# The S5 recurrence of a Trainium2 block kernel: 15 powered steps replaced by a turned scan, and its output work moved to earlier stages

## What is computed

```python
G, P = 32, 64                                   # channel groups of 16, complex states
dt = jnp.exp(log_dt)[:, None]; mag = jnp.exp(dt * a_re)
abar_re, abar_im = mag * cos(dt * a_im), mag * sin(dt * a_im)
...                                             # bbar = coef * b, complex
bu_re = jnp.einsum("gpc,btgc->tbgp", bbar_re, ug); bu_im = ...
# s[t] = abar * s[t-1] + bu[t], complex, over the 512 tokens
_, _, s_re, s_im = lax.associative_scan(_ssm_combine, (a_seq_re, a_seq_im, bu_re, bu_im), axis=0)
y = einsum("gcp,tbgp->btgc", c_re, s_re) - einsum("gcp,tbgp->btgc", c_im, s_im) + d_skip * ug
zz = gelu(y)
out = zz * sigmoid(zz @ w_glu + b_glu)          # 512 x 512 weights
y_s5 = rms_norm(out) * gain
mix = concatenate([y_rwkv, y_s5]) @ w_out       # 1024 x 1024
```

## Time and profile before

| | us |
|---|---|
| median of 3 runs | 1648.43 (1647.06 to 1651.15) |
| the profiled execution | 1645.37 |
| its span in the trace | 1643.6 |
| busy in the span: TensorE / VectorE / ScalarE / GpSimd | 1492.7 / 805.6 / 584.4 / 269.5 |
| mean granted TensorE clock | 0.959 |

### The profile page before, as it was taken

How to read it: one execution, slowest core, us unless ns; L and a number is a source line. 1 busy time by engine, 2 the same in 40 slices (tenths; PEclk the granted TensorE clock), 3 DMA queues, 4 the chain that set the end, 5 groups by cost and what they waited for, 6 DMA issues and landing times.

```text
span 1643.6 us, 23774 instructions
## 1 busy us (share of the span) xinstructions
PE 1492.7 (91%) x10032; PEld 1155.1 (70%) x10032; DVE 805.6 (49%) x1255; ACT 584.4 (36%) x1012; POOL 269.5 (16%) x225
## 2 busy tenths in 40 slices
PE   6998897987899999999988999988898899998899
PEld 3676675875688888888766777666676677766667
DVE  7766855245543323223445554356534655435652
ACT  4265231245333222322333434134523343323441
POOL 0000232001001101100012332222101233222210
PEclk9999999998899999999989999999998999999999
DMA  9258242521222232332311121201222112120121
GB/s 376 71 116 109 70 171 106 165 83 44 72 90 90 90 103 90 104 121 92 119 47 39 52 77 53 76 26 52 72 95 84 39 52 78 51 77 26 52 90 64
DMA packets 51369, 143.12 MB, mean 87 GB/s; under 512 B 13248, under 2 KB 17984, under 8 KB 50496
## 3 DMA queue, kind: packets, MB, share of 16 engines
q1 hardware_dynamic: 51264, 141.60, 27.2%
HBM read 136.90 MB, written 4.69 MB: 86 GB/s over the span
## 4 chain that ended last, share of the span: by engine, by line
PE 72%; DVE 12%; ACT 8%; issue 3%; POOL 1%; DMA 1%; SPq 1%; DVEq 0%; ACTq 0%
PE b L394 71%; ACT arena L2148 5%; DVE arena L1260 2%; DVE ring L1260 2%; DVE arena L1268 2%; PE b L397 1%; ACT ring L2151 1%; POOL arena L2793 1%; DVE arena L1978 1%; ACT L2148 1%; ACT arena L2151 1%; DVE X L1260 1%; DVE arena L2111 1%; ACT tile L2151 1%; DVE arena L1936 1%
## 5 line engine op out<-in xcount | busy, mean ns | idle before, releaser
L394 PE MATMUL b<-tile,ring 128*128 128x512 f32 x2288 | 702.4, 401 | 14.8 <-ACT tile L2151 7.7
L394 PE MATMUL b<-HR,ring 128*128 128x512 f32 (+1 forms) x1888 | 625.1, 407 | 62.9 <-DVE ring L1260 34.9
L394 PEld LDWEIGHTS b<-tile,ring 128*128 128x128 f32 x2288 | 435.1, 191 | 122.4 <-issue 14.3
L394 PEld LDWEIGHTS b<-HR,ring 128*128 128x128 f32 (+1 forms) x1888 | 363.1, 192 | 163.9 <-issue 61.6
L1260 DVE TENSOR_TENSOR ring<-ring,ring 128x1024 fp32r<-128x1024 f32 x186 | 254.8, 1372 | 298.6 <-ACT ring L2151 294.8
L2151 ACT ACTIVATE ring<-ring 128x1024 fp32r<-128x1024 f32 x186 | 195.6, 1054 | 210.2 <-PE b L394 210.2
L394 PE MATMUL b<-arena 64*64 64x64 f32 (+10 forms) x3104 | 232.2, 286 | 26.4 <-issue 9.7
L394 PEld LDWEIGHTS b<-arena 64*64 64x64 f32 (+5 forms) x3104 | 149.3, 149 | 98.1 <-issue 70.6
L1260 DVE TENSOR_TENSOR arena<-arena 128x512 f32<-128x512 f32 (+7 forms) x206 | 110.7, 569 | 74.8 <-ACT arena L2148 53.7
L2151 ACT ACTIVATE arena<-b 128x512 f32<-128x512 f32 (+2 forms) x146 | 78.2, 559 | 193.2 <-PE b L394 153.2
L2793 POOL TENSOR_SCALAR arena<-arena 128x128 f32<-128x128 f32 (+1 forms) x64 | 87.1, 1377 | 209.0 <-DVE arena L1983 209.0
(11 more groups left out here) (117 smaller groups left out, 985.7 us busy)
## 6 DMA issues: line engine op xcount, KB each, us to landing
ring<-in_ws SPq DMA_DIRECT2D x218, 512.0 KB, 3.5
arena<-in_ws SPq DMA_DIRECT2D x15, 512.0 KB, 15.3
arena<-in_lw SPq DMA_DIRECT2D x2, 1280.0 KB, 5.5
X<-in_xT SPq DMA_DIRECT2D x2, 1024.0 KB, 6.3
arena<-scr_kpad SPq DMA_DIRECT2D x8, 256.0 KB, 11.5
X<-in_xT SPq DMA_DIRECT2D x1, 2048.0 KB, 8.0
outT<-X SPq DMA_DIRECT2D x8, 256.0 KB, 2.0
arena<-in_cst SPq DMA_DIRECT2D x1, 1088.0 KB, 5.0
```

Of the source, the lines that this page charges most:

```text
L394: return self.e.matmul(out, lhsT, rhs, start=start, stop=stop, skip_group_check=True)
```

## The change

VectorE has an instruction that runs s[t] = a[t] * s[t-1] + b[t] along a row (the trace's `TENSOR_TENSOR_SCAN`), for real numbers. With abar^8 = m8 (c8 + i s8), the contribution e[j] is turned back by the angle times j (multiplied with cos, -sin of it), so that the recurrence has the real factor m8, is scanned, and the states are turned forward again.

- `s5_tables`: the table of 8 powers of abar^8 goes (2 copies and 18 small operations); m8, c8, s8 come from three squarings (18 small operations), ahead of the `PR`, `PI` powers. It has other yields, so VectorE's table work falls elsewhere between weight splits.
- `turn_tables`, new, right after `extra_tables`: cos and sin of the angle times 0 to 63 by six doublings, each 4 + 2 operations on 128 x 16 x (1, 2, 4, 8, 16, 31), and the factor row of 1024, zeroed where a group begins.
- `s5_apply` on VectorE: for each half 6 operations on 128x512 that read the e banks directly (ScalarE's four copies go), two scans of 128x1024, then for each half 6 operations of 128x512. All 14 steps and the wide step go.
- The strings: the e matmuls come one unit earlier (before z6), the states are ready in the z stage, the `yg` matmuls stand after z10 and after z11, the round trip ahead of the grams' ada loads, Gelu, hi and lo in the inverse's first level, `glu` between the inverse's levels, the square sums ahead of "steps". `OZ` has its own region, and the S5 rows of the output projection can be made before group norm ends.
- Waits: z10's shift and the second half of RWKV's scaling wait for the states; `ada_evict` 2 waits for yg 1; the gate's sigmoid for the columns 5. The first of the group norm's tables is loaded by ScalarE before the last chunk's copy (c == 7).

```diff
 U_TILES = [14, 15, 16, 17]
-PREP = "zpzzpz" + "smzpm" + "szpmzp" + "sssss" + "zps" + "zpss" + "zpss" + "zps" + "zps"
-MIX = ("rrrrarrrrarrrrra" + "ssssrrrrrrrra" + "sssrrrrrrrra" + "srrrrsrrrra" + "srrsrrsrrsrra" + "srrrrrrrra"
-       + "rrrrasrrrrs" + "rgsrgsrsrsrrsrsr" + "ogooog")
+PREP = "zpzzpz" + "smzpmm" + "szp" + "sszssp" + "sszp" + "szp" + "szp" + "zpss" + "zssp"
+MIX = ("s" + "rrarsrrarrarrrrrra" + "rrrrsrrrraa" + "rrrrarrrra" + "rrrrasrrrrs" + "rrrrsrrrrs" + "rrrrsrrrrs"
+       + "rrrrsrrrr" + "rgrgrrrrrr" + "goooog")
...
-        self.P8R, self.P8I = R(127.125, 8, 16), R(127.625, 8, 16)
...
-        self.carry = [self.ring2f[:, o:o + 784].rearrange("p (g b i) -> p g b i", b=7, i=7) for o in (2048, 2832)]
+        self.rot, self.decay, self.rtemp = R(36, 2, 16, 64), R(48, 16, 64), R(20, 2, 512)
...
-        self.LL, self.PP = self.ring2f[:, 0:2048].rearrange("p (a t) -> p a t", a=4), R(68, 4, 512)
+        self.LL, self.PP = self.H[:, 0:4, :], R(68, 4, 512)
...
-        for ri in range(2):
-            for h in range(2):
+        for h in range(2):
+            for ri in range(2):
...
-                self.give(("e", ri, h), (act, ("e", ri, h)))
-                yield
-        for _ in range(1 + 7 + 7 + 2):
+                self.give(("e", ri, h), (k.s("s5_dve"), ("turned", h)))
+            yield
+        for _ in range(1 + 5):
             yield
...
+        for m, c, s in ((mag, cs, sn), (m8, c8, s8), (m8, c8, s8)):
+            self.wait_ge(tab, SOFAR)
+            V(u1, c, c, ALU.mult)
+            V(u2, s, s, ALU.mult)
+            V(u3, c, s, ALU.mult)
+            V(m8, m, m, ALU.mult)
+            self.wait_ge(tab, SOFAR)
+            V(c8, u1, u2, ALU.subtract)
+            S(s8, u3, 2.0, ALU.mult)
+        yield
...
-        self.cp(P8R[:, 0, :], PR[:, :, 8]).then_inc(*tab.inc())
-        self.cp(P8I[:, 0, :], PI[:, :, 8]).then_inc(*tab.inc())
-        tm2 = k.region(83, 4, 4, 16)
-        for lo, n in ((1, 1), (2, 2), (4, 4)):
-            bb = lambda ap: ap.unsqueeze(1).broadcast_to((128, n, 16))
-            ar_, ai_ = bb(P8R[:, lo - 1, :]), bb(P8I[:, lo - 1, :])
-            br_, bi_ = P8R[:, 0:n, :], P8I[:, 0:n, :]
-            self.wait_ge(tab, SOFAR)
-            for i, (p, q_) in enumerate(((br_, ar_), (bi_, ai_), (br_, ai_), (bi_, ar_))):
-                V(tm2[:, i, 0:n, :], p, q_, ALU.mult)
-            self.wait_ge(tab, SOFAR)
-            V(P8R[:, lo:lo + n, :], tm2[:, 0, 0:n, :], tm2[:, 1, 0:n, :], ALU.subtract)
-            V(P8I[:, lo:lo + n, :], tm2[:, 2, 0:n, :], tm2[:, 3, 0:n, :], ALU.add)
-            yield
...
+    def turn_tables(self):
+
+        k = self.k
+        tab = k.s("tab")
+        re, im = k.rot[:, 0], k.rot[:, 1]
+        c8, s8, m8 = k.sm[18:21]
+
+        def V(out, a, b, op):
+            self.tt(out, a, b, op).then_inc(*tab.inc())
+        self.wait_ge(tab, SOFAR)
+        self.e.memset(re[:, :, 0], 1.0).then_inc(*tab.inc())
+        self.e.memset(im[:, :, 0], 0.0).then_inc(*tab.inc())
+        self.cp(re[:, :, 1], c8).then_inc(*tab.inc())
+        self.cp(im[:, :, 1], s8).then_inc(*tab.inc())
+        for lo, n in ((1, 1), (2, 2), (4, 4), (8, 8), (16, 16), (32, 31)):
+            bc = lambda ap: ap[:, :, lo].unsqueeze(2).broadcast_to((128, 16, n))
+            t = [k.region(44 + 2 * i, 16, 32)[:, :, 0:n] for i in range(4)]
+            self.wait_ge(tab, SOFAR)
+            V(t[0], re[:, :, 1:1 + n], bc(re), ALU.mult)
+            V(t[1], im[:, :, 1:1 + n], bc(im), ALU.mult)
+            V(t[2], re[:, :, 1:1 + n], bc(im), ALU.mult)
+            V(t[3], im[:, :, 1:1 + n], bc(re), ALU.mult)
+            self.wait_ge(tab, SOFAR)
+            V(re[:, :, lo + 1:lo + 1 + n], t[0], t[1], ALU.subtract)
+            V(im[:, :, lo + 1:lo + 1 + n], t[2], t[3], ALU.add)
+        self.wait_ge(tab, SOFAR)
+        self.cp(k.decay, m8.unsqueeze(2).broadcast_to((128, 16, 64))).then_inc(*tab.inc())
+        self.wait_ge(tab, SOFAR)
+        self.e.memset(k.decay[:, :, 0], 0.0).then_inc(*tab.inc("rot"))
+
...
         if n == 10:
             self.wait_ge(k.s("kpad", 16), "k")
+            self.wait_ge(k.s("s5_dve"), "states")
...
         self.extra_tables()
+        self.turn_tables()
...
+        for _ in range(2 + 2 + 1):
+            yield
+        flat = lambda ap: ap.rearrange("p g j -> p (g j)")
+        half = lambda ap, h: flat(ap[:, 8 * h:8 * h + 8, :])
+        T1, T2 = k.rtemp[:, 0, :], k.rtemp[:, 1, :]
+        self.wait_ge(k.s("kpad", 16), "k")
+        self.wait_ge(k.s("tab"), "rot")
+        self.wait_ge(k.s("ud", 16), 0)
+        for h in range(2):
+            re, im, C, D = half(S[:, 0], h), half(S[:, 1], h), half(k.rot[:, 0], h), half(k.rot[:, 1], h)
+            er, ei = k.bank["e", 0, h][:, :], k.bank["e", 1, h][:, :]
+            self.wait_ge(pe, ("e", 1, h))
+            if h:
+                self.wait_ge(dve, SOFAR)
+            V(T1, er, C, ALU.mult)
+            V(re, ei, D, ALU.mult)
+            V(T2, er, D, ALU.mult)
+            V(im, ei, C, ALU.mult, ("turned", h))
             self.wait_ge(dve, SOFAR)
-            V(dst, dst, T1, ALU.add)
+            V(re, re, T1, ALU.add)
+            V(im, im, T2, ALU.subtract)
+            yield
+        self.wait_ge(dve, SOFAR)
+        for ri in range(2):
+            x = flat(S[:, ri])
+            self.e.tensor_tensor_scan(out=x, data0=flat(k.decay), data1=x, initial=0.0,
+                                      op0=ALU.mult, op1=ALU.add).then_inc(*dve.inc())
+        yield
+        for h in range(2):
+            re, im, C, D = half(S[:, 0], h), half(S[:, 1], h), half(k.rot[:, 0], h), half(k.rot[:, 1], h)
             self.wait_ge(dve, SOFAR)
-            V(dst[:, 0], dst[:, 0], T2[:, 1], ALU.subtract)
-            V(dst[:, 1], dst[:, 1], T2[:, 0], ALU.add, *events)
+            V(T1, re, D, ALU.mult)
+            V(T2, im, D, ALU.mult)
             self.wait_ge(dve, SOFAR)
-        Sv = S.rearrange("p r g (b i) -> p r g b i", i=8)
-        T = [k.region(129.75 + i, 2, 16, 8) for i in range(2)]
-        power = lambda ap, n: ap.unsqueeze(1).unsqueeze(3).broadcast_to((128, 2, 16, n))
-        for ri in range(2):
-            for h in range(2):
-                self.wait_ge(act, ("e", ri, h))
-        for i in range(1, 8):
-            step(Sv[:, :, :, :, i], Sv[:, :, :, :, i - 1], power(k.P8R[:, 0, :], 8), power(k.P8I[:, 0, :], 8), *T)
-            yield
-        for b in range(1, 8):
-            step(Sv[:, :, :, b, 7], Sv[:, :, :, b - 1, 7], k.P8R[:, 7, :].unsqueeze(1).broadcast_to((128, 2, 16)),
-                 k.P8I[:, 7, :].unsqueeze(1).broadcast_to((128, 2, 16)), T[0][:, :, :, 0], T[1][:, :, :, 0])
-            yield
-        T = k.carry
-        ends = [Sv[:, ri, :, 0:7, 7].unsqueeze(3).broadcast_to((128, 16, 7, 7)) for ri in (0, 1)]
-        power = lambda ap: ap[:, 0:7, :].rearrange("p i g -> p g i").unsqueeze(2).broadcast_to((128, 16, 7, 7))
-        self.wait_ge(k.s("dense"), ("in", 11))
-        for ri, op in ((0, ALU.subtract), (1, ALU.add)):
-            rest = Sv[:, ri, :, 1:8, 0:7]
+            V(re, re, C, ALU.mult)
+            V(im, im, C, ALU.mult)
             self.wait_ge(dve, SOFAR)
-            V(T[0], ends[ri], power(k.P8R), ALU.mult)
-            V(T[1], ends[1 - ri], power(k.P8I), ALU.mult)
-            self.wait_ge(dve, SOFAR)
-            V(rest, rest, T[0], ALU.add)
-            self.wait_ge(dve, SOFAR)
-            V(rest, rest, T[1], op, *(["states"] if ri else []))
-            yield
-        for _ in range(4 + 1):
-            yield
-        YS, Z = k.YS, k.Z
+            V(re, re, T2, ALU.subtract)
+            V(im, im, T1, ALU.add, *(["states"] if h else []))
+            yield
+        for _ in range(4 + 2):
+            yield
+        Z = k.YS
...
-        if k.order[8 * u][0] == "glu":
-            self.wait_ge(k.s("inv_pe"), ("p", 4, 3))
-            self.wait_ge(k.s("s5_dve"), "states")
...
+        if g == 2:
+            self.wait_ge(k.s("s5_pe"), ("yg", 1))
...
-        for ri in range(2):
-            for h in range(2):
-                self.wait_ge(pe, ("e", ri, h))
-                self.wait_ge(k.s("ud", 16), 0)
-                self.cp(k.S[:, ri, 8 * h:8 * h + 8, :].rearrange("p a j -> p (a j)"),
-                        k.bank["e", ri, h][:, :]).then_inc(*act.inc(("e", ri, h)))
-                yield
-        for _ in range(1 + 7 + 7 + 2):
+        for _ in range(2 + 1 + 5):
...
+            self.wait_ge(k.s("cols_pe"), 5)
+            self.af(k.OZ[:, n, :], k.bank["glu", n][:, :], ACT.Sigmoid,
...
+            if c == 7:
+                self.af(k.nst[:, 570:571], k.kc(EPS6), ACT.Ln)
```

More of the change, by code:

```diff
@@ L249, in views @@
         self.w2, self.g2 = R(88.125, 512), R(24, 512)
-        self.YS, self.Z, self.GQ = R(92, 4, 512), R(100, 4, 512), R(84, 4, 512)
-        self.OS, self.OZ = self.YS, self.Z
+        self.YS, self.GQ = R(92, 4, 512), R(84, 4, 512)
+        self.OS, self.OZ = self.YS, R(100, 4, 512)
```

(37 more changed lines are left out.)

10 lines of the change are left out of this document (3 added, 7 removed).

## The result

The changed kernel takes 1657.42 us (median of 7 runs, 1653.33 to 1660.11), the one before 1647.06 (7 runs, 1645.53 to 1651.15): ratio 1.0057, 95% interval 1.004 to 1.0073. The forecast was 1628, the range 1612 to 1643. The profiled execution took 1654.12 with a span of 1652.3; it is compared with the one of before, whose span is 1643.6: +8.7.

The account below looks back on a forecast made before the run. TensorE's work stays the same, so only its waits and low-clock stretches count: 8.5 - 10.1 - 8.3 - 0.8 - 9.9 = -20.6 us on 1645.4, giving a median of 1628; range 1612 to 1643.

Parts of the forecast that it names:

- Start-up, turn tables, turns and scans: Start-up and z stage: VectorE's tables and recurrence delay splits, less old waits that go; +8.5 us in sum.
- 7.4 of the 9.5, since glu's 48 matmuls stand where a level waited for its results: Inverse: glu's matmuls fill levels that wait for their own results, removing 7.4 of 9.5 us of waits.
- 4.1 of low clock: Inverse: 4.1 us of low clock go, part of the stage's -10.1.
- 2.9: Scan: 2.9 us of low clock in its window go, part of -8.3.
- Steps, -8.3: Before steps: VectorE's lateness from square sums and Gelu's chain goes (5.4), with the scan's low clock (2.9): -8.3 us.
- Grams at 0: Grams stage: no change in time forecast, 0 us.
- The lo halves, 4.0: Inverse's first level: TensorE newly waits for VectorE's lo halves, 4.0 us with 1.7 of low clock.
- The rule weighed: Inverse's first level: the lo halves could wait for POOL's masks, up to 2.5 us more; nothing added to the sum.
- Scan: Scan: TensorE sets its pace, not the scan's own chain, so the glu time taken out counts in full.
- Group norm: Behind the scan: sums start earlier and S5 matmuls fill the unchanged chain; -9.9 us (-6 to -12).
- (c): Rival: VectorE becomes the bound in the z stage, at twice the price of its operations; 1659 us, chance 0.05.
- (d): Rival: the inverse's gain returns as waits for ada loads and group norm's chain; within 5 of 1648, chance 0.07.

Follow-up runs that it names:

- Experiment 12: Changed kernel with three more products (2.8 us of TensorE) in the inverse's third level, just ahead of the 4.0 us wait: 1654.68 us, ratio 1.0032.
- experiment 9: Kernel before with three quarters of the yg matmuls left out of the inverse: 1639.56 us, ratio 0.9959.
- experiment 5: Changed kernel with the 2 MB input reload issued behind the glu weights' loads instead of ahead of them: 1650.49 us, ratio 1.0007.
- experiment 4: Changed kernel with S5's norm on VectorE moved from ahead of the scan's inputs into the scan's chunks, its halves behind it: 1649.96 us, ratio 1.0011.
- experiment 6: Changed kernel with splits ahead of the scans, S5's norm in the scan and the input reload behind the glu weights: 1642.03 us, ratio 0.9961.
- experiment 10: Changed kernel with turns, scans and turning back on an eighth of their columns: 1639.25 us, ratio 0.995.
- experiment 7: Changed kernel with ada weights from the third group on loaded only in 128 of 1024 columns: 1643.07 us, ratio 0.9972.
- experiment 8: Kernel before with ada weights from the third group on loaded only in 128 of 1024 columns: 1638.53 us, ratio 0.9945.
- experiment 1: Changed kernel with VectorE's order alone altered, weight splits ahead of the two scans and of the turning back: 1649.32 us, ratio 1.001.
- experiment 11: Changed kernel with splits ahead of the scans, norm in the scan, late reload, and ada columns spread: 1643.66 us, ratio 0.9978.

## Why the prediction was wrong, by its own steps

- **Start-up, turn tables, turns and scans**: right in mechanism and nearly in size, +10.6 for +8.5. Tables, turns and scans took what was forecast; the waits were 3.9, 7.5 and 4.1 for 3.8, 7.8 and 3.7. Start-up was +2.6 at the first wait and, with more low clock, +3.8 where the z stage begins, for +3.1; behind z10's split 2.7 us went to low clock where I had 1.0. These make most of the rest.
- **Inverse, "7.4 of the 9.5, since glu's 48 matmuls stand where a level waited for its results"**: this step failed. The waits are not for results but for packets of TensorE's own instructions, each lasting 128 small matmuls or 2.1 us; they stand where the count ends, so a filler at the end of a level meets them by chance only. Experiment 12 shows it for the wait of 4.0, and the times of the packets for the seven of 0.3 us and more in the inverse. Instead of falling from 9.5 to 2.1 they grew to 11.7. Why they grew is shown in part: yg, which gave the queue time, went (1.6 us in experiment 9, in the kernel before), and the reload of the input runs beside the wait of 4.0 (1.7 us less without it in experiment 5, though other waits took that back).
- **Inverse, "4.1 of low clock"** and **"2.9" in the scan**: the sum took waits and low clock to vanish together. As waits stayed, half clock stayed: 6.8 us lost between grams and scan, and 3.4 in the scan (clock 0.88). Where a wait did go, it went too: behind the scan's start in experiments 4 and 6, and in the z stage in experiment 10.
- **Steps, -8.3**: what made VectorE late was taken away, but the sum did not carry the norm's four operations, which the same letters put ahead of the scan's first inputs: 3.4 us and 3.4 of clock, given back by experiment 4.
- **Grams at 0**: three ada groups stand closer than their loads allow; +3.0. In the inverse I had 3.0 for one such pair, and 2.0 of waits and 2.8 of longer groups more than before came. By experiments 7 and 8 the loads explain about 3 us of the difference between the kernels.
- **The lo halves, 4.0**: not seen; 2.6, for the additions that stand behind them on VectorE, where the wait for instructions in front was shorter (experiment 7: 1.4 instead of 2.8).
- **The rule weighed, that VectorE and GpSimd lock each other out of a shared pair of ports** (the Trainium skill, "SBUF — State Buffer", "SBUF: two separate sides"): the lo halves took 2.50 us as before, starting 2.4 us after the masks had ended; no run put the two together, and the sum's choice stands. The doubling itself was read from unlike rows: the 4.01 of the earlier trace rows are two multiplications, the first mostly ahead of the masks, the 1.98 two additions. The additions beside the masks, which compare with the 1.98, took 3.90:

```profile
260.32 3.90 DVE L1260 TENSOR_TENSOR X<-X,ring2f 128x784 f32<-128x784 f32 x2
```

- **Scan**: right; without glu it takes 25.1 us, TensorE-bound. **Group norm**: right in mechanism, -7.6 of -9.9. The first sum came at 1.4 us behind the scan's end (2.5 forecast), but from it to the last wait it was 24.4 us and not 21.1: 1.7 of low clock, and a chain of 22.7 us also where there was none (experiments 4 and 6).
- The rivals: (c), slower because VectorE is the bound in the z stage, had the right sign, and its 1659 lies 2 us from the measured 1657.4, but by chance: it needs operations at twice their price, and they took what was forecast. VectorE's work did cost 15 us there (experiment 10), which the forecast had nearly in full. (d) is closest to what happened in mechanism, though its 1648 was too low: what was won came back in the inverse, in other waits than named.

Open: why experiment 1 wins 8 us in the median and 4 in the profile; and how the runs of one kernel come to differ by 7 us and more. In experiment 11 it is mostly granted clock: the slowest run had 0.953 and the fastest 0.959, some 10 of the 11.7 us between them by an estimate from these means. In experiment 4 it is not: 0.954 and 0.957, some 6 of 16.9 us.
